# Two transformer blocks on one core: the RMS norms' sums, root and reciprocal in quarters, and the residual's add on VectorE

## The chip, the cores and the metric

One core of one Trainium2 chip. The metric is the device time of one execution in microseconds. The kernel before took 3231.95, 3235.20 and 3235.36 us in three runs, median 3235.2. All numbers of the trace come from one more execution, taken by the profiler.

## What is computed

The input is 1024 tokens of width 1024, all in fp32. The first block is an RWKV-7 mixer joined with differential attention, its output projection, a norm behind it, the residual, and a feed-forward with a short convolution between a norm before and a norm behind. The second block is a forgetting attention and a banded attention with gates, an output projection, a norm, and a feed-forward with a squared ReLU; a last norm ends it. What the change touches is the RMS norm over the 1024 features of a token:

```python
def rms_norm(x, g, eps=NORM_EPS):
    x32 = x.astype(jnp.float32)
    y = x32 * lax.rsqrt(jnp.mean(x32 * x32, axis=-1, keepdims=True) + eps)
    return (y * g.astype(jnp.float32)).astype(x.dtype)
...
        h = h + rms_norm(mix @ w_out[l], ln_attn_post[l])
        hn = rms_norm(h, ln_ffn_pre[l])
...
        h = h + rms_norm(f, ln_ffn_post[l])
```

## The kernel before

**Layout.** Activations lie feature-major: eight tiles (`KT`) of 128 features by 1024 tokens. A linear layer works in units: one unit is 128 output features, products over eight contraction tiles, 48 matmuls of 512 tokens, into one pair of PSUM banks (`bank2(slot)`; the two slots alternate, so unit n waits until unit n-2 is read out: `evac_done`). fp32 products are made of three matmuls on split operands: a rounded high part (`wh`, `xh`) and the rest (`wl`, `xl`), `three_products`, L359. For each unit SyncE loads a weight tile (`load_w`), ScalarE rounds it (`split_hi`, L330) and GpSimd subtracts (`split_lo`, L337), two units ahead at most.

**A norm's statistics.** There are six, numbered k = 0 to 5: before the first block (0), behind its output projection (1), before its feed-forward (2), behind it (3), before the second block (4), before the second feed-forward (5). Squares come from ScalarE (`square_act`, into `sq`). The sum over features is made in two ways. In 0, 2 and 4 TensorE multiplies each tile of squares by a 128x128 matrix of ones as it comes (`square_sum_pe`, L374) into banks 6 and 7, where every partition then holds the sums of all 1024 tokens. In 1, 3 and 5 VectorE adds the eight tiles into `ss` (`square_sum_dve`, L384) and TensorE multiplies `ss` once (`stat_products`, L415). ScalarE takes the root over 128x1024 (`stat_root_act`, L423) and VectorE the reciprocal in place (`stat_reciprocal`, L430), giving `rstd`. It is applied only when a unit is evacuated, or in a post norm to `y`.

**The post norms** (1 and 3) with the pre norm that follows (2 and 4) are one pipeline over eight tiles. VectorE multiplies `y` by gain and `rstd` (`post_scale`, L2265); GpSimd adds the residual tile `hres` into `src` (`post_norm_pool`, L2283), two buffers; ScalarE rounds it with the next gain into `xh` and squares it (`prep_act`, L394), and its queue issues the store of the new residual; VectorE makes `xl` (`prep_dve`, L404); SyncE loads `hres` two tiles ahead once an add is done (`post_norm_loads`, L2290). The add waits for the tile's scaling, the load, the store that still reads its buffer, and the low half and the square of two tiles before. TensorE runs the first unit of the next layer at the pace of the tiles, a tile's squares ahead of its products; the second unit follows whole. After the first pipeline GpSimd clears `y` by eight memsets, each after its add, before the feed-forward adds into it, and then splits the third unit's weights.

**Order.** Each engine's queue is written out by hand and is worked off in order; waits are on semaphores. After norm 4 the forget gate's unit (`U_FA`) is evacuated first and a chain of small operations on VectorE and ScalarE follows (L3102 to L3115) before the next unit's evacuation and weight split. Norm 5's products come behind a whole unit; the next two units have the transposes of the residual among their tiles (`turn_residual`, L2353), in banks 4 to 7.

Of the kernel before, what the change touches and what calls it, by code (L numbers as in the profile page):

```python
# [10 lines left out]
ALU = mybir.AluOpType  # L11
# [3 lines left out]
P = 128  # L15
T = 1024
D = 1024
# [92 lines left out]
def build_program(nc, a, out):  # L110
    ctx = ExitStack()
    with ctx:
# [20 lines left out]
        ones = at("ones", 205.75, [P, P])  # L133
# [7 lines left out]
        ss = at("ss", 200, [P, T])  # L141
        y = at("y", 112, [P, KT, T])
# [154 lines left out]
        stat_sum = sem("stat_sum")  # L297
        stat_root = sem("stat_root")
        rstd_ready = sem("rstd_ready")
# [115 lines left out]
        def stat_products(pe, sums):  # L415

            pe.wait_ge(ss_done, sums)
            for h in range(2):
                mm = nc.tensor.matmul(ps[:, 6 + h, :], ones[:, :], ss[:, h * HALF:(h + 1) * HALF],
                                      start=True, stop=True)  # L420
            mm.then_inc(stat_sum, 1)

        def stat_root_act(act, k, sums=None):  # L423


            act.wait_ge(*((ss_done, KT * (k + 1)) if sums is None else (stat_sum, sums)))
            nc.scalar.activation(rstd[:, :], bank2(3), ACT.Sqrt, bias=small[:, 0:1], scale=1.0 / D)\
                .then_inc(stat_root, 1)

        def stat_reciprocal(dve, k):  # L430
            dve.wait_ge(stat_root, k + 1)
            nc.vector.reciprocal(rstd[:, :], rstd[:, :]).then_inc(rstd_ready, 1)
            dve.wait_ge(rstd_ready, k + 1)
# [1829 lines left out]
        def post_scale(dve, kt, gain):  # L2263

            nc.vector.scalar_tensor_tensor(out=y[:, kt, :], in0=y[:, kt, :], scalar=col(gain, kt), in1=rstd[:, :],  # L2265
                                           op0=ALU.mult, op1=ALU.mult).then_inc(scaled, 1)

        def post_norm(dve, post_gain, r0, q0, pre_gain):
            post_scale(dve, 0, post_gain)
            for kt in range(KT):  # L2270
                if kt + 1 < KT:
# [926 lines left out]
```

## Time and profile before

| | |
|---|---|
| median of three runs | 3235.2 us |
| profiled execution, its own time | 3235.84 us |
| its span, first to last instruction | 3234.1 us |
| mean granted TensorE clock | 0.985 |
| busy: PE, PEld, DVE, ACT, POOL | 94%, 76%, 48%, 30%, 21% |
| the chain that ended last, share by engine | PE 83%, DVE 7%, issue 5%, ACT 2% |
| weights' high half on ScalarE (L335), mean | 1060 ns |
| weights' low half on GpSimd (L340), mean | 2444 ns |

PE is TensorE's matmuls, PEld its weight loads, DVE VectorE, ACT ScalarE, POOL GpSimd, SP SyncE. A row of a timeline gives the start, the length, engine, line, operation, output and inputs, shapes, count, and in brackets how long the engine was idle before it and what released it. Several instructions of one kind stand in one row, and the length then runs from the first start to the last end. The granted clock is a share of the full 2.4 GHz; 0.5 is the lower level of 1.2 GHz.

### The profile page before, as it was taken

The page shows a single profiled execution, that of the slowest core. Times are in us where ns is not written, and L with a number is a line of the kernel's source. Part 1 is how long each engine was busy: PE and PEld are TensorE (multiplying, and loading weights), DVE is VectorE, ACT ScalarE, POOL GpSimd, SP SyncE. Part 2 cuts the span into 40 slices and gives each one's busy share as a digit, 9 for nine tenths or more (in the row PEclk, how much of TensorE's full clock was granted, in tenths as well). Part 3 has the DMA queues.
Part 4 walks back from the last instruction along what each step waited for, and adds up shares of the span by engine and source line. Part 5 has one row for each costly group of instructions (what it writes and reads, how often), then busy time and mean ns, then how long its engine had stood idle before and what let it go on. Part 6 is the DMA issues. An engine that isn't in the chain of part 4 may idle for free.

```text
span 3234.1 us, 48488 instructions
## 1 busy us (share of the span) xinstructions
PE 3054.6 (94%) x20334; PEld 2444.8 (76%) x20334; DVE 1558.9 (48%) x1868; ACT 968.9 (30%) x1434; POOL 678.8 (21%) x292
## 2 busy tenths in 40 slices
PE   7999988889799999999799999999899999999998
PEld 5877767767488888888578877766688888888887
DVE  4156668741754444455731134555454444444455
ACT  3145545532322222222331133344332211111112
POOL 2410121212422122222243410000022221222221
PEclk9999999999899999999899999999899999999999
DMA  4443330021321111111243633344544411111111
GB/s 171 141 134 105 118 107 25 24 69 52 130 65 46 45 39 59 51 46 40 86 146 122 195 109 126 118 135 125 201 139 130 137 33 52 52 52 52 42 36 65
DMA packets 233982, 292.77 MB, mean 91 GB/s; under 512 B 10057, under 2 KB 182226, under 8 KB 233818
## 3 DMA queue, kind: packets, MB, share of 16 engines
q1 hardware_dynamic: 218842, 243.22, 24.5%
q10 hardware_dynamic: 14976, 47.19, 3.8%
q8 instruction: 124, 2.03, 0.3%
q14 instruction: 40, 0.33, 0.0%
HBM read 209.86 MB, written 80.51 MB: 90 GB/s over the span
## 4 chain that ended last, share of the span: by engine, by line
PE 83%; DVE 7%; issue 5%; ACT 2%; DMA 1%; POOL 1%; SPq 0%; DVEq 0%; ACTq 0%; POOLq 0%
PE ps L363 61%; PE ps L1331 4%; PE ps L1901 4%; PE ps L488 4%; PE ps L1971 2%; PE ps L1952 2%; PE ps L1929 1%; PE ps L1394 1%; DVE xl L404 1%; POOL src L2283 1%; PE ps L1932 1%; DVE y L2401 1%; DVE cb L2506 1%; PE ps L380 0%; PE ps L1372 0%
## 5 line engine op out<-in xcount | busy, mean ns | idle before, releaser
L340 POOL TENSOR_TENSOR wl<-wraw,wh 128x1024 fp32r<-128x1024 f32 x151 | 369.0, 2444 | 1638.1 <-ACT wh L335 1638.1
L363 PE MATMUL ps<-xh,wh 128*128 128x512 f32 x2192 | 686.4, 394 | 7.0 <-POOL xl L1169 2.2
L363 PE MATMUL ps<-xl,wh 128*128 128x512 f32 x2192 | 677.0, 390 | 0.0
L363 PE MATMUL ps<-xh,wl 128*128 128x512 f32 x2192 | 676.9, 390 | 0.0
L363 PEld LDWEIGHTS ps<-xh,wh 128*128 128x128 f32 x2192 | 412.4, 189 | 105.0 <-issue 8.1
L363 PEld LDWEIGHTS ps<-xl,wh 128*128 128x128 f32 x2192 | 413.2, 189 | 86.3
L363 PEld LDWEIGHTS ps<-xh,wl 128*128 128x128 f32 x2192 | 412.7, 188 | 86.3
L335 ACT ACTIVATE wh<-wraw 128x1024 fp32r<-128x1024 f32 x167 | 177.0, 1060 | 960.4 <-PE ps L363 894.3
L2401 DVE TENSOR_TENSOR y<-ps,y 128x1024 f32<-128x1024 f32 x208 | 253.2, 1222 | 241.6 <-PE ps L363 241.4
L2311 POOL TENSOR_TENSOR dl<-draw,dh 128x2048 fp32r<-128x2048 f32 x25 | 119.1, 4765 | 519.3 <-ACT dh L2307 519.3
L2448 DVE SCALAR_TENSOR_TENSOR cb<-ub,cols,cb 128x1024 f32<-128x1024 f32 x88 | 127.0, 1443 | 61.8 <-ACT cb L2484 56.0
L363 PE MATMUL ps<-dh,fh 128*128 128x512 f32 x480 | 149.3, 392 | 6.0 <-DVE y L2401 6.0
L363 PE MATMUL ps<-dh,fl 128*128 128x512 f32 x480 | 147.9, 389 | 0.0
L363 PE MATMUL ps<-dl,fh 128*128 128x512 f32 x480 | 147.9, 389 | 0.0
L2438 DVE TENSOR_TENSOR ub<-ps,rstd 128x1024 f32<-128x1024 f32 x44 | 53.9, 1225 | 172.7 <-PE ps L363 172.5
L2506 DVE TENSOR_TENSOR cb<-ps,rstd 128x1024 f32<-128x1024 f32 x32 | 39.2, 1225 | 193.4 <-PE ps L363 193.2
L2095 DVE CUSTOM_DVE_ANT_0 pbuf<-ps,bias 128x640 f32<-128x640 f32 (+7 forms) x128 | 85.5, 705 | 97.1 <-PE ps L1937 49.4
L2307 ACT ACTIVATE dh<-draw 128x2048 fp32r<-128x2048 f32 x25 | 47.8, 1913 | 235.2 <-PE ps L363 235.2
L1952 PE MATMUL ps<-ident,pbuf 128*128 128x128 f32 x528 | 94.0, 287 | 20.4 <-DVE pbuf L2151 9.8
L363 PEld LDWEIGHTS ps<-dh,fh 128*128 128x128 f32 x480 | 89.0, 188 | 29.4 <-DVE y L2401 11.5
L1952 PEld LDWEIGHTS ps<-ident,pbuf 128*128 128x128 f32 x528 | 60.9, 143 | 59.5 <-DVE pbuf L2151 17.3
L363 PEld LDWEIGHTS ps<-dh,fl 128*128 128x128 f32 x480 | 90.1, 188 | 18.9
(336 smaller groups left out, 4526.4 us busy)
## 6 DMA issues: line engine op xcount, KB each, us to landing
wraw<-in_w_up SPq DMA_DIRECT2D x76, 512.0 KB, 3.9
wraw<-in_w_in SPq DMA_DIRECT2D x67, 512.0 KB, 4.1
draw<-in_w_down SPq DMA_DIRECT2D x27, 1024.0 KB, 5.0
residual<-src ACTq DMA_DIRECT2D x32, 512.0 KB, 4.9
proj<-stage SPq DMA_DIRECT2D x30, 512.0 KB, 2.9
qk_hi<-hs ACTq DMA_DIRECT2D x24, 512.0 KB, 2.7
qk_lo<-ls SPq DMA_DIRECT2D x24, 512.0 KB, 2.8
kh<-qk_hi SPq DMA_DIRECT2D x48, 256.0 KB, 7.1
```

The lines of the kernel that those rows point to most:

```text
L335: nc.scalar.activation(wh[:, s, :, :], wraw[:, s, :, :], ACT.Copy).then_inc(w_hi, 1)
L340: nc.gpsimd.tensor_tensor(wl[:, s, :, :], wraw[:, s, :, :], wh[:, s, :, :].bitcast(F32), ALU.subtract).then_inc(w_lo, 1)
L363: mm = nc.tensor.matmul(ps[:, bank + h, :], w, x[:, h * HALF:(h + 1) * HALF], start=start and k == 0, stop=stop and k == 2)
L488: return nc.tensor.matmul(to, left, right, **kw)
L1331: ins = mm(ps[:, 2 * fill_slot(u) + h, :], w[:, s, kt, :], x[:, kt, h * HALF:(h + 1) * HALF], start=kt == 0 and part == 0, stop=kt == KT - ...
L1901: ins = mm(ps[:, 6 + h, :], w[:, s, kt, :], x[:, kt, h * HALF:(h + 1) * HALF], start=kt == 0 and part == 0, stop=kt == KT - 1 and part == 2)
L1952: ins = nc.tensor.transpose(ps[:, bank, (k - 4 * g) * P:(k - 4 * g + 1) * P], pbuf[:, (TT * b + n) % 3, m, k * P:(k + 1) * P], ident[:, :])
L2095: a2_dve.done(nc.vector.tensor_tensor_reduce(pbuf[:, step % 3, m, 0:size], ps[:, 2 * m:2 * m + 2, :].rearrange("p a n -> p (a n)")[:, 0:size],
L2311: nc.gpsimd.tensor_tensor(dl[:, :, :], draw[:, :, :], dh[:, :, :].bitcast(F32), ALU.subtract)\
L2401: nc.vector.tensor_tensor(y[:, m, :], bank2(2 + m % 2), y[:, m, :], ALU.add).then_inc(down_added, 1)
L2448: ff1_dve.done(nc.vector.scalar_tensor_tensor(out=cb[:, r, :], in0=ub[:, r, 2 - back:T + 2 - back], scalar=col_at("conv_w", (2 - back) * 2 ...
L2506: nc.vector.tensor_tensor(cb[:, 0, :], bank2((U_UP2 + t) % 2), rstd[:, :], ALU.mult)\
```

## The change

Sums: the ones become 128x32. Each tile of squares is multiplied in four matmuls of 256 tokens, each into its own 32 partitions of one bank (bank 4), so that partitions 32q to 32q+31 hold the sums of the q-th quarter of the tokens. Root and reciprocal then work on 128x256 (`root`). Two matrices with two rows of ones each, used by halves of 64 partitions, spread the quarters back to all partitions in banks 6 and 7 (`spread_pe`); in norms 0, 2, 4 and 5 ScalarE copies that to `rstd`, in the post norms VectorE multiplies from PSUM. In norms 1, 3 and 5 VectorE adds seven of the eight tiles; TensorE adds the last one in the bank. The residual's add, now with the post gain, moves from GpSimd to VectorE. Half of the second unit's tiles are issued among the first unit's. In norm 1 one weight split of ScalarE is moved behind the last square, in norm 2 one ahead of the copy. GpSimd's memsets wait for all sixteen low halves.

```diff
-        ones = at("ones", 205.75, [P, P])
+        spread_even = at("spread_even", 205.75, [P, P])
+        spread_odd = at("spread_odd", 207, [P, P])
+        ones = at("ones", 207.5, [P, 32])
+        root = at("root", 200, [P, T // 4])
...
+        STAT_BANK = 4
+        QUARTERS = [slice(32 * q, 32 * q + 32) for q in range(4)]
+        QUARTER_TOKENS = [slice(q * T // 4, (q + 1) * T // 4) for q in range(4)]
+        def quarter_sums(of, start, stop):
+            for q in range(4):
+                mm = nc.tensor.matmul(ps[QUARTERS[q], STAT_BANK, 0:T // 4], ones[:, :], of[:, QUARTER_TOKENS[q]],
+                                      start=start, stop=stop)
+            return mm
         def square_sum_pe(pe, q):
             if q and q % KT == 0:
                 pe.wait_ge(stat_root, q // KT)
             pe.wait_ge(x_sq, q + 1)
-            for h in range(2):
-                mm = nc.tensor.matmul(ps[:, 6 + h, :], ones[:, :], sq[:, q % 2, h * HALF:(h + 1) * HALF],
-                                      start=q % KT == 0, stop=q % KT == KT - 1)
-            mm.then_inc(ss_done, 1)
+            quarter_sums(sq[:, q % 2, :], q % KT == 0, q % KT == KT - 1).then_inc(ss_done, 1)
+        def post_sums_pe(pe, q):
+            pe.wait_ge(stat_root, q // KT)
+            pe.wait_ge(ss_done, q + KT - 1)
+            quarter_sums(ss, True, False)
+            pe.wait_ge(x_sq, q + KT)
+            quarter_sums(sq[:, 1, :], False, True).then_inc(ss_done, 1)
+        spread = bank2(3)
+        def spread_pe(pe, k):
+            pe.wait_ge(rstd_ready, k + 1)
+            for w, half in ((spread_even, 0), (spread_odd, 1)):
+                for r in range(2):
+                    mm = nc.tensor.matmul(ps[:, 6 + r, half * T // 4:(half + 1) * T // 4], w[ROWS[r], :], root[ROWS[r], :],
+                                          start=True, stop=True)
+            mm.then_inc(spread_done, 1)
+        def rstd_copy_act(act, k):
+            act.wait_ge(spread_done, k + 1)
+            nc.scalar.activation(rstd[:, :], spread, ACT.Copy).then_inc(rstd_copied, 1)
...
-            nc.scalar.activation(rstd[:, :], bank2(3), ACT.Sqrt, bias=small[:, 0:1], scale=1.0 / D)\
+            nc.scalar.activation(root[:, :], ps[:, STAT_BANK, 0:T // 4], ACT.Sqrt, bias=small[:, 0:1], scale=1.0 / D)\
...
-            nc.vector.reciprocal(rstd[:, :], rstd[:, :]).then_inc(rstd_ready, 1)
+            nc.vector.reciprocal(root[:, :], root[:, :]).then_inc(rstd_ready, 1)
+        def paced_units(pe, n, s, r0, q0, k):
...
+            for kt in range(KT):
+                square_sum_pe(pe, q0 + kt)
...
+                pe.wait_ge(x_lo, r0 + kt + 1)
+                mm = products(0, kt)
...
+                if 3 <= kt < KT - 1:
+                    products(1, kt - 3)
+            mm.then_inc(mm_done, 1)
+            for kt in range(4, KT):
+                if kt == 6:
+                    spread_pe(pe, k)
+                mm = products(1, kt)
+            mm.then_inc(mm_done, 1)
...
+        def post_scale(dve, kt):
+            nc.vector.tensor_tensor(y[:, kt, :], y[:, kt, :], spread, ALU.mult).then_inc(scaled, 1)
+        def post_add(dve, k, kt, gain, r0, q0):
+            s = kt % 2
+            dve.wait_ge(scaled, KT * k + kt + 1)
+            dve.wait_ge(h_loaded[s], 16 * (4 * k + kt // 2 + 1))
+            dve.wait_ge(x_lo, r0 + kt - 1)
+            dve.wait_ge(x_sq, q0 + kt - 1)
+            dve.wait_ge(src_stored[s], 16 * ((r0 + kt) // 2))
+            nc.vector.scalar_tensor_tensor(out=src[:, s, :], in0=y[:, kt, :], scalar=col(gain, kt), in1=hres[:, s, :],
+                                           op0=ALU.mult, op1=ALU.add).then_inc(added, 1)
+        def post_norm(dve, k, post_gain, r0, q0, pre_gain):
+            dve.wait_ge(spread_done, 2 * k + 2)
+            post_scale(dve, 0)
             for kt in range(KT):
+                post_add(dve, k, kt, post_gain, r0, q0)
                 if kt + 1 < KT:
-                    post_scale(dve, kt + 1, post_gain)
+                    post_scale(dve, kt + 1)
                 prep_dve(dve, r0 + kt, q0 + kt, pre_gain)
...
-            post_norm_pool(pool, 0, 8, 16)
+            pool.wait_ge(x_lo, 16)
             for kt in range(KT):
-                pool.wait_ge(added, kt + 1)
                 nc.gpsimd.memset(y[:, kt, :], 0.0).then_inc(y_zero, 1)
...
             stat_root_act(act, 0)
+            rstd_copy_act(act, 0)
...
-                split_hi(act, n + 2, n % 2)
+                if kt < KT - 1:
+                    split_hi(act, n + 2, n % 2)
...
-            stat_root_act(act, 1, 1)
+            split_hi(act, U_UP + 1, 1)
+            stat_root_act(act, 1)
             post_norm_act(act, 0, 8, 16, "ln_ffn_pre")
             stat_root_act(act, 2)
-            ff1_act_chunk(act, 0, 0)
+            split_hi(act, U_UP + 2, 0)
+            rstd_copy_act(act, 2)
+            ff1_act_chunk(act, 0, 0, begun=True)
...
+            stat_root_act(act, 4)
             split_hi(act, U_FA + 2, U_FA % 2)
-            stat_root_act(act, 4)
+            rstd_copy_act(act, 4)
...
-            for s in range(2):
-                unit_products(pe, s, s, 0, first=True)
+            unit_products(pe, 0, 0, 0, first=True)
+            unit_products(pe, 1, 1, 0, first=True, before=lambda kt: spread_pe(pe, 0) if kt == 4 else None)
...
-            stat_products(pe, 16)
-            unit_products(pe, U_UP, 0, 8, before=lambda kt: square_sum_pe(pe, 16 + kt))
-            for k in range(1, 4):
+            post_sums_pe(pe, 8)
+            spread_pe(pe, 1)
+            paced_units(pe, U_UP, 0, 8, 16, 2)
+            for k in range(2, 4):
                 unit_products(pe, U_UP + k, k % 2)
...
-            stat_products(pe, 32)
-            unit_products(pe, U_FA, 0, 16, before=lambda kt: square_sum_pe(pe, 32 + kt))
+            post_sums_pe(pe, 24)
+            spread_pe(pe, 3)
+            paced_units(pe, U_FA, 0, 16, 32, 4)
...
-            stat_products(pe, 48)
+            post_sums_pe(pe, 40)
+            def among(k, kt):
+                if k == 1 and kt == 2:
+                    spread_pe(pe, 5)
+                if kt % 2:
+                    turn_residual(pe, 4 * k - 4 + kt // 2)
...
+            for k, w in enumerate((spread_even, spread_odd)):
+                nc.vector.memset(w[:, :], 0.0).then_inc(spread_set, 1)
+                dve.wait_ge(spread_set, 3 * k + 1)
+                for r in range(2):
+                    row = 64 * r + 32 * k
+                    nc.vector.memset(w[row:row + 1, :], 1.0).then_inc(spread_set, 1)
```

In norm 5 `turn_residual` waits for the root before its first tile and for ScalarE's copy of the spread before its second. Where a norm's `rstd` is copied, VectorE waits for the copy (`rstd_copied`) behind its reciprocal.

## Rows read from the trace of the kernel before

**Rows 1.** The page's costliest groups, TensorE's first: busy, mean ns | idle before, releaser
```profile
L363 PE MATMUL ps<-xh,wh 128*128 128x512 f32 x2192 | 686.4, 394 | 7.0 <-POOL xl L1169 2.2
```

**Rows 2.** Busy time by stretch: PE, PEld, DVE, ACT, POOL (x), PEclk, DMA share, GB/s
```profile
804.40:826.60 22.20, 3.79 (x5) 1.18 (x4) 10.54 (x5) 5.36 (x6) 6.91 (x3) 0.58 0.02 1
...
826.60:859.00 32.40, 25.43 (x71) 14.03 (x72) 28.55 (x14) 15.56 (x15) 20.79 (x10) 0.92 0.80 269
...
863.60:874.50 10.90, 10.90 (x50) 9.03 (x49) 9.18 (x6) 2.31 (x2) 2.47 (x2) 1.00 0.17 50
```

**Rows 3.** Timeline, 806 to 827 us, all engines: start, length [idle before <-releaser]
```profile
807.59 1.47 DVE L392 TENSOR_TENSOR ss<-ss,sq 128x1024 f32<-128x1024 f32 x1 [9.34 <-ACT sq L372]
...
809.12 3.78 PE L419 MATMUL ps<-ss,ones 128*128 128x512 f32 x4 [4.71 <-DVE ss L392]
...
812.94 1.11 ACT L427 ACTIVATE rstd<-ps,small 128x1024 f32<-128x1024 f32 x1 [5.38 <-PE ps L419]
...
814.09 6.55 DVE L432 RECIPROCAL rstd<-rstd 128x1024 f32<-128x1024 f32 x1 [5.02 <-ACT rstd L427]
...
822.04 5.63 POOL L2283 TENSOR_TENSOR src<-y,hres 128x1024 f32<-128x1024 f32 x2 [14.05 <-DVE y L2265]
...
826.57 2.18 DVE L404 SCALAR_TENSOR_TENSOR xl<-src,cols,xh 128x1024 fp32r<-128x1024 f32 x1 [3.41 <-ACT xh L398]
```

**Rows 4.** Prices: durations ns min/median/max, a group's mean, and four timeline pieces
```profile
L979 DVE RECIPROCAL kb<-kb x16: 1694/1742/1753, 431.7 to 625.2; 128x256 f32<-128x256 f32 x16
...
L2081 ACT ACTIVATE pt<-ps 128x256 f32<-128x256 f32 x12 | 4.6, 385 | 20.6 <-PE ps L1952 20.6
...
L2438 DVE TENSOR_TENSOR ub<-ps,rstd x44: 1217/1225/1226, 870.1 to 1527.7; 128x1024 f32<-128x1024 f32 x44
...
L2265 DVE SCALAR_TENSOR_TENSOR y<-y,cols,rstd x16: 1270/1282/3398, 820.7 to 1617.1; 128x1024 f32<-128x1024 f32 x16
...
2520.08 1.88 PE L419 MATMUL ps<-ss,ones 128*128 128x512 f32 x4
...
1949.54 3.46 PE L1971 MATMUL ps<-pt,vt 128*64 128x256 f32 x32
...
471.63 0.69 PE L512 MATMUL ps<-wa,lora_w 64*128 64x512 f32 x1 [2.62 <-DMA lora_w<-in_w_iclr_up]
...
471.64 0.69 PE L517 MATMUL ps<-wa,lora_w 64*128 64x512 f32 x1
...
472.17 0.59 PE L512 MATMUL ps<-wa,lora_w 64*128 64x512 f32 x1
```

**Rows 5.** Timeline of TensorE and VectorE, 1576 to 1626 us
```profile
1576.65 3.78 PE L419 MATMUL ps<-ss,ones 128*128 128x512 f32 x4 [3.78 <-DVE ss L392]
...
1594.10 2.18 DVE L404 SCALAR_TENSOR_TENSOR xl<-src,cols,xh 128x1024 fp32r<-128x1024 f32 x1 [3.41 <-ACT xh L398]
...
1620.58 4.79 DVE L404 SCALAR_TENSOR_TENSOR xl<-src,cols,xh 128x1024 fp32r<-128x1024 f32 x2
```

**Rows 6.** Timeline at the loop of 826 us; releasers of the residual's adds (us, times)
```profile
857.74 1.28 DVE L404 SCALAR_TENSOR_TENSOR xl<-src,cols,xh 128x1024 fp32r<-128x1024 f32 x1 [3.45 <-ACT xh L398]
...
835.13 2.96 POOL L2283 TENSOR_TENSOR src<-y,hres 128x1024 f32<-128x1024 f32 x1 [1.76 <-DMA residual<-src]
...
  DMA residual<-src: 7.5, 3
```

**Rows 7.** Timeline behind the two loops: GpSimd, VectorE, TensorE
```profile
856.48 7.19 POOL L2773 MEMSET y<- 128x1024 f32 x8
...
1637.56 1.21 DVE L3102 TENSOR_TENSOR fa<-ps,rstd 8x1024 f32<-8x1024 f32 x1
...
1652.12 0.72 PE L363 MATMUL ps<-xh,wh 128*128 128x512 f32 x2 [1.57 <-DVE stage L3122]
```

**Rows 8.** The chain that ended last, 22 to 50 us: start, length, what
```profile
32.10 1.98 PE ps L380 x4
...
34.09 0.89 PE ps L2939 x8
```

More of the change, by code:

```diff
@@ L413, in apart, with stat_root_act @@
             eng.sem_inc(marks, 1)
[L415 to L426, printed above, removed]
-            nc.scalar.activation(rstd[:, :], bank2(3), ACT.Sqrt, bias=small[:, 0:1], scale=1.0 / D)\
+        def stat_root_act(act, k):
+            act.wait_ge(ss_done, KT * (k + 1))
+            nc.scalar.activation(root[:, :], ps[:, STAT_BANK, 0:T // 4], ACT.Sqrt, bias=small[:, 0:1], scale=1.0 / D)\
                 .then_inc(stat_root, 1)
@@ L2260, in build_program @@
         out_stored = sem("out_stored")
[L2263 to L2269, printed above, removed]
+        def post_scale(dve, kt):
[12 more added lines that the diff above has]
+            post_scale(dve, 0)
             for kt in range(KT):
+                post_add(dve, k, kt, post_gain, r0, q0)
                 if kt + 1 < KT:
-                    post_scale(dve, kt + 1, post_gain)
+                    post_scale(dve, kt + 1)
                 prep_dve(dve, r0 + kt, q0 + kt, pre_gain)
-        def post_norm_pool(pool, k, r0, q0):
-            for kt in range(KT):
-                s = kt % 2
-                pool.wait_ge(scaled, KT * k + kt + 1)
-                pool.wait_ge(h_loaded[s], 16 * (4 * k + kt // 2 + 1))
-                pool.wait_ge(x_lo, r0 + kt - 1)
-                pool.wait_ge(x_sq, q0 + kt - 1)
-                pool.wait_ge(src_stored[s], 16 * ((r0 + kt) // 2))
-                nc.gpsimd.tensor_tensor(src[:, s, :], y[:, kt, :], hres[:, s, :], ALU.add).then_inc(added, 1)
         def post_norm_act(act, k, r0, q0, pre_gain):
@@ L2408, in down_add @@
                         square_sum_dve(dve, squares + m - 1)
-            if squares is not None:
-                square_sum_dve(dve, squares + KT - 1)
         def y_squares_act(act, d, q0):
@@ L2930, in _ @@
             pe.wait_ge(lam_dve, 3)
-            nc.tensor.matmul(ps[:, 4, 0:1], ones[0:1, :], lam_dots[:, 2:3], start=True, stop=True).then_inc(lam_pe, 1)
+            pe.wait_ge(spread_set, 6)
+            nc.tensor.matmul(ps[:, 4, 0:1], spread_even[0:1, :], lam_dots[:, 2:3], start=True, stop=True).then_inc(lam_pe, 1)
+            pe.wait_ge(lam_dve, 4)
             for s in range(2):
@@ L3075, in _ @@
                 rwkv_dve(dve, j)
-            for kt in range(KT):
+            for kt in range(KT - 1):
                 square_sum_dve(dve, 8 + kt)
             stat_reciprocal(dve, 1)
-            post_norm(dve, "ln_attn_post", 8, 16, "ln_ffn_pre")
+            post_norm(dve, 0, "ln_attn_post", 8, 16, "ln_ffn_pre")
             stat_reciprocal(dve, 2)
+            dve.wait_ge(rstd_copied, 2)
             for s in range(2):
```

45 lines of the change are left out of this document (31 added, 14 removed).

## The prediction

> **What bounds the kernel now.** I read the page first. In [rows 1] TensorE's largest group of products waited 7.0 us in all over the whole span, so almost everywhere TensorE works without a gap, and only a change in TensorE's own work or in its few gaps can move the end. Next I asked for busy time by stretch at the norms. In [rows 2] the stretch from 804.4 to 826.6 us, after the last product of the output projection, has TensorE busy for 3.79 of 22.2 us; the next, to 859.0, has 25.43 of 32.4; and the one from 863.6 to 874.5, a whole unit, has 10.90 of 10.90. A unit is thus 10.9 us, one of its eight contraction tiles 1.36 us. The same shape comes back after the first block's feed-forward. So the change is argued in five places: the start, the two post norms with the pre norms that follow them, the fifth norm's tail, and the sixth norm.
>
> **The lead of a post norm.** The timeline [rows 3] is one chain, each row released by the one before. Products end at 804.41 (809.12 less its idle 4.71). ScalarE then splits a weight (1.06, its mean in the table of the profile), copies the tile and squares it, VectorE adds the last squares (807.59 to 809.06), TensorE sums over partitions (four passes, 3.78 us, so 0.94 each), ScalarE takes the root (1.11), VectorE the reciprocal (6.55), then scales; GpSimd adds the residual (two in 5.63 us); ScalarE rounds; the first low half starts at 826.57.
>
> The new prices. Reciprocal of 128x256: 1.74 us [rows 4]. Root from PSUM of 128x256: a ScalarE copy of that form takes 0.39; I take 0.45. Scaling from PSUM without a gain: 1.22. The add with gain on VectorE: 1.28, the undisturbed time of its form; that row's maximum, 3.40, belongs to instructions beside GpSimd's adds, which are gone. For the sums there is no 32-column row. Full-width plain fp32 takes 0.47 us per 512 columns at full clock (four passes in 1.88); eight passes of 256 are the same columns, so 1.9 us is the bound if the tiles do not run side by side. With 64-column tiles 32 passes took 3.46 us, 28 of them of 256 columns and four of 128; at the full-width rate the 7680 columns would take 7.1. Two tiles therefore do run beside each other, and four would give 0.45. I take 0.6 us with the last pass's latency, 1.1 at the low clock, near the lower end because of that factor of two. A gain below 0.45 is excluded by the streaming of 512 columns per tile. For the spread, the two 64-row tiles start together and the next pair follows 0.54 us later for 512 columns [rows 4]; four pairs of 256 lie between 1.1 (half of that each) and 2.2 (no gain from the halved width, weight loading binding), serial 1.9. I take 1.2 at the high level and 2.2 at the low one.
>
> Chain of the first post norm, from 804.41: with the weight split moved behind, ScalarE copies from 804.5 and squares until 806.6 (the add of 807.59 followed the square's old end; 1.0 earlier now). VectorE's seven earlier adds are in the bank already; TensorE adds the last tile, to 807.8. ScalarE is at the moved split until 807.6, so the root runs to 808.3, the reciprocal to 810.05, the spread to 812.3 (TensorE stood idle, and in the old lead it ran its sums at 0.94 us a pass), scaling to 813.6, the add to 814.9, rounding to 816.06. First low half at 816.1 against 826.57: **10.5 us** saved.
>
> Here a rule speaks against the change. No row shows a switch costing more than fractions of a microsecond: the 3.46 us above have full-width passes straight before and behind. The Trainium skill, TensorEngine Tiling (Array Packing), Key Properties, says that changing the tiling mode drains TensorE. By the rule each norm tile gets two drains more; by the row they cost under 0.2 us each and lie in TensorE's slack of the tile loop, so the sum stays as it is.
>
> Second post norm [rows 5]: products end at 1572.87 (1576.65 less 3.78). The eighth VectorE add ended at 1576.6, so the seventh, one of 1.3 us before it, at about 1575.3, as it still will, then two sets of sums (1577.3), root 1577.8, reciprocal 1579.6, spread 1581.8, scale 1583.1, add 1584.4, first low half 1585.6 against 1594.10: **8.5 us**.
>
> **The tile loop.** Before, from the start of the first low half to the end of the last: 826.57 to 859.02 and 1594.10 to 1625.37, or 32.4 and 31.3 us [rows 3, 5, 6]. In the new order VectorE does add, scale of the next tile, low half. The low half waits for ScalarE's rounding: add 1.28 + hand-over 0.04 + rounding 1.15 + 0.04, then 1.2 until the next add starts, so 3.7 us a tile; without that wait three operations would give 3.55. Seven of these and one low half: 27.2 us. Saved: **5.3 and 4.1 us**. What hides there: TensorE's sums (0.6) and one or two contraction tiles (1.36 or 2.72), at most 3.3 of 3.7. GpSimd is out of it. SyncE's loads of the residual now wait for VectorE's add, its issues and those of ScalarE's stores are as many as before. Their limit: a store issued at an add's end let the add two tiles later start 5.1 to 7.4 us on [rows 6]: the add at 835.13 waited 1.76 for a transfer issued at the end of the second add, 822.04 + 5.63 [rows 3]. At 3.7 a tile I allow 6.0; the 7.4 came from two stores and two loads issued within 2.4 us, so I take 5 to 6 and keep 7.4 as a bound (4.4 a tile).
>
> **The tails.** Call T the end of the last low half. Before, the first unit ended at 863.6, so TensorE started the third unit at 874.5, T + 15.45. Now four of the second unit's contraction tiles were done in the loop; left are the last sums (the last square ends at T - 0.3, the sums at 0.4), its tile (1.75), two tiles (4.5), the spread (5.7; root at 0.9 and reciprocal at 2.7 are ready by then), two tiles: T + 8.4. ScalarE's copy of the spread and VectorE's first evacuation end at 8.1. But GpSimd's eight memsets (7.19 us, [rows 7]) now wait for all sixteen low halves, where before they began with the last add, and the split of the third unit's weights (2.44, the mean in the table of the profile) is queued behind them: T + 9.75. That becomes the new bound, a TensorE wait of 1.3 us on GpSimd. Saved: **5.7 us**.
>
> At the second block the tail was from 1625.37 to 1652.12. It hangs on the forget-gate chain: its first multiply on VectorE at 1637.56, the third unit 14.56 later [rows 7]. The multiply now comes after the spread and its copy, T + 6.85, so the unit at T + 21.4 instead of T + 26.75: **5.3 us**. TensorE waits some 2 us there.
>
> **Start.** The loop over two tiles is copy, rounding, squares, sums 1.98, transposes 0.89 [rows 8], 6.3 us; with sums of 0.6 some 5.1, where VectorE (5.0: two copies of 1.23, two low halves of 1.28) and ScalarE (4.4: two of 1.15, two of 1.04) follow close. Two such periods give 2.4, the first tiles and the last sums 2 to 3, the spread inside the second unit costs 1.2, and a lower clock in the looser loop would take it all back (sums 1.1, transposes 1.8: 6.6 us). Between -1.5 and +5; I take **+2.5**. The added wait of ScalarE for the spread holds its weight split for the third unit back to some 19.7 us into the pair of units, low half 22.2, needed at 23.0: covered, narrowly. VectorE's six small memsets lie before the input's arrival.
>
> **Sixth norm.** One set of sums (1.75 as it delays the products, [rows 4]: 1.88) becomes two of 0.5 and a spread of 1.2: **-0.4**. Its ScalarE copy delays a weight split by about 3 us, with some 6 us to spare. Waiting for the copy before the second turned tile costs at most 0.3.
>
> **Sum.** 10.5 + 5.3 + 5.7 = 21.5; 8.5 + 4.1 + 5.3 = 17.9; + 2.5 - 0.4: 41.5 us. The profiled execution took 3235.84 us, 1.74 more than its span, and 0.6 above the runs' median of 3235.2; taken from it, 3194.3, so 3194.
>
> **Rivals.**
> - *The transfers bound the tile loops.* 4.4 us a tile instead of 3.7: 14 x 0.7 = 9.8 us less gain, 3204. For: the DMA engines' share was 0.80 at 269 GB/s in the old loop [rows 2], and 3.7 us a tile wants some 285. Against: only three adds of sixteen waited for transfers [rows 6], at the loops' beginnings, where two tiles followed each other closely. 15%.
> - *The 32-column tiles run one after the other*, the change not doing what it says. Sums then cost 1.9 (3.8 low): 2.7 and 5 more in the leads, four tiles a loop at 4.6 instead of 3.7 (7.2 in both), 1.3 each in the tails and 2.8 at the sixth norm, and the gain at the start is gone (2.5): 23 us less, 3217. The 64-column row speaks against. 10%.
> - *Slower.* Every switch between full-width, column-tiled and row-tiled matmuls stalls TensorE. About 60 switches; some 44 are not covered (the start's 16, the crowded tiles of the loops, leads and tails). It decides from 0.95 us each; at 1.2 the time is 3235.8 - 41.5 + 53 = 3247. The rows bound a switch at 0.2. It would be seen as gaps around the narrow passes. 3%, and 2% for no change.
> - 70% for the forecast, whose own range is 3186 to 3202: the start's -1.5 to +5, the spreads' bounds, 3.55 to 3.9 us a tile.
>
> A measurement of this kernel tells 0.2% (6.5 us) from no change. Faster: 0.95. The range takes in the forecast and the DMA rival with its own spread: 3184 to 3209; left out is mostly the serial case.
>
> **What would show it.** Right: low halves 3.6 to 3.8 us apart, the first ones 11.7 and 12.7 us after the products' end; narrow sums of about 0.6 us; a wait of TensorE on GpSimd's split behind the memsets; the third unit 36 to 37 us after the first low half. Wrong: sums of 1.9 us; VectorE's adds released by the residual's transfers; granted clock under 0.8 in the loops; a start loop still at 3.1 us a tile.

## The result, and the profile after

The changed kernel took 3197.68 us (median of four runs, 3195.33 to 3198.89); the kernel before, run beside it, 3233.57 (3228.49 to 3235.36). The ratio is 0.9891, interval 0.9874 to 0.9908. The profiled execution took 3198.89 us with a span of 3197.2 us and a mean granted clock of 0.987. The forecast was 3194: faster, as foreseen, and by 36.9 us between the two profiled spans where the sum was 41.5. One execution of the kernel before, beside the second set of the changed one, took 6135 us at full clock; it is left out of every comparison, and what held it up is not known.

Three names are used from here on. A *lead* runs from the end of the products in front of a post norm to the start of the first low half (`xl`, VectorE); a *loop* from there to the end of the last of the eight low halves, a moment called T; a *tail* from T to TensorE's third unit, or to that unit's counterpart in the second block.

First the stretches that answer to [rows 2]: busy time of PE, PEld, DVE, ACT, POOL, granted clock, DMA share and GB/s, in the lead, the tile loop and one unit behind it.

```profile
805.50:816.70 11.20, 3.27 (x24) 1.41 (x24) 5.42 (x5) 4.61 (x6) 2.34 (x1) 0.67 0.03 5
816.70:843.90 27.20, 23.75 (x130) 14.21 (x130) 25.40 (x21) 15.57 (x15) 0.00 (x0) 0.88 0.91 297
854.60:865.50 10.90, 10.90 (x50) 9.02 (x49) 8.50 (x6) 4.42 (x4) 2.53 (x1) 1.00 0.34 98
```

The lead of 22.2 us is 11.2, the loop of 32.4 is 27.2, and VectorE is now busy for 25.4 of those 27.2: with ScalarE's rounding, which stands between a tile's add and its low half, it sets the pace. Next the timeline of the lead, which answers to [rows 3]; products end at 805.48.

```profile
805.42 0.64 PE L386 MATMUL ps<-ss,ones 128*32 128x256 f32 x8
...
806.58 1.06 ACT L377 ACTIVATE sq<-y 128x1024 f32<-128x1024 f32 x1
...
807.69 0.64 PE L386 MATMUL ps<-sq,ones 128*32 128x256 f32 x8 [1.63 <-ACT sq L377]
808.49 0.45 ACT L455 ACTIVATE root<-ps,small 128x256 f32<-128x256 f32 x1
...
808.98 1.75 DVE L460 RECIPROCAL root<-root 128x256 f32<-128x256 f32 x1 [9.64 <-ACT root L455]
...
810.78 1.22 PE L412 MATMUL ps<-root,spread_even 64*128 64x256 f32 x4 [2.45 <-DVE root L460]
...
811.80 1.06 PE L412 MATMUL ps<-root,spread_odd 64*128 64x256 f32 x4
812.90 1.22 DVE L2319 TENSOR_TENSOR y<-y,ps 128x1024 f32<-128x1024 f32 x1 [2.18 <-PE ps L412]
814.16 1.28 DVE L2329 SCALAR_TENSOR_TENSOR src<-y,cols,hres 128x1024 f32<-128x1024 f32 x1
...
815.48 1.15 ACT L435 ACTIVATE xh<-src,cols 128x1024 fp32r<-128x1024 f32 x1 [6.54 <-DVE src L2329]
...
816.66 1.28 DVE L441 SCALAR_TENSOR_TENSOR xl<-src,cols,xh 128x1024 fp32r<-128x1024 f32 x1
```

The chain is the foretold one. Eight narrow passes take 0.64 us (at full clock), the root 0.45, the reciprocal 1.75 where the wide one took 6.55, the spread 2.08 at the low level. The first low half starts 11.18 us after the products' end; 11.7 was forecast.

Behind the loop, T is 843.85. The timeline of GpSimd and TensorE there, and then of the second block, where T is 1592.71:

```profile
843.91 7.23 POOL L2828 MEMSET y<- 128x1024 f32 x8 [32.92 <-DVE xl L441]
851.10 2.39 POOL L345 TENSOR_TENSOR wl<-wraw,wh 128x1024 fp32r<-128x1024 f32 x1
...
853.54 0.73 PE L368 MATMUL ps<-xh,wh 128*128 128x512 f32 x2 [1.05 <-POOL wl L345]
```

```profile
1585.22 1.28 DVE L2329 SCALAR_TENSOR_TENSOR src<-y,cols,hres 128x1024 f32<-128x1024 f32 x1 [1.01 <-DMA residual<-src]
...
1599.51 1.21 DVE L3183 TENSOR_TENSOR fa<-ps,rstd 8x1024 f32<-8x1024 f32 x1 [4.15 <-ACT rstd L419]
...
1611.96 2.32 DVE L3203 SCALAR_TENSOR_TENSOR stage<-ps,rstd 128x1024 f32<-128x1024 f32 x2
...
1614.32 0.72 PE L368 MATMUL ps<-xh,wh 128*128 128x512 f32 x2 [2.10 <-DVE stage L3203]
```

TensorE's unit starts at T + 9.69 after a wait of 1.05 us for GpSimd, and at T + 21.61 after one of 2.10 for the evacuation behind the forget-gate chain. In the second loop one add waited 1.01 us for a store of the residual.

All figures are us; a minus is a loss.

| step | before | after | saved | forecast |
|---|---|---|---|---|
| first lead (products' end to first low half) | 22.17 | 11.18 | 11.0 | 10.5 |
| first loop | 32.45 | 27.19 | 5.3 | 5.3 |
| first tail (T to the unit's start) | 15.45 | 9.69 | 5.8 | 5.7 |
| second lead | 21.23 | 11.86 | 9.4 | 8.5 |
| second loop | 31.27 | 28.29 | 3.0 | 4.1 |
| second tail | 26.75 | 21.61 | 5.1 | 5.3 |
| start (VectorE's evacuation near 90 us) | 90.29 | 88.59 | 1.7 | 2.5 |
| sixth norm (its last low half's end to the end of the span) | 720.0 | 720.4 | -0.4 | -0.4 |

The last row starts at the end of these low halves, 2514.10 before and 2476.74 after:

```profile
2511.85 2.25 DVE L404 SCALAR_TENSOR_TENSOR xl<-src,cols,xh 128x1024 fp32r<-128x1024 f32 x1 [1.22 <-ACT xh L398]
```

```profile
2474.50 2.24 DVE L441 SCALAR_TENSOR_TENSOR xl<-src,cols,xh 128x1024 fp32r<-128x1024 f32 x1 [1.22 <-ACT xh L435]
```

The rows give 11.0 + 5.3 + 5.8 + 9.4 + 3.0 + 5.1 + 1.7 - 0.4 = 40.9 us; the spans differ by 36.9. The missing part lies where the change has no line: 2.8 us from VectorE's evacuation near 90 us to the end of the output projection's products, 0.6 between the first tail and the second lead, and 0.4 between the second tail and the sixth norm. Windows over the same instructions in the first attention, before and after (columns as above):

```profile
249.50:257.20 7.70, 7.39 (x45) 5.84 (x45) 3.93 (x10) 4.50 (x13) 0.00 (x0) 1.00 0.06 18
296.90:324.00 27.10, 24.72 (x142) 19.23 (x142) 18.00 (x58) 17.17 (x44) 2.36 (x1) 1.00 0.13 40
```

```profile
247.80:257.10 9.30, 9.01 (x45) 7.11 (x45) 3.92 (x10) 4.48 (x13) 0.00 (x0) 0.82 0.05 15
296.80:325.40 28.60, 26.21 (x142) 20.31 (x142) 17.98 (x57) 17.10 (x43) 2.40 (x1) 0.94 0.13 38
...
1614.30:1627.10 12.80, 12.78 (x49) 10.43 (x50) 0.00 (x0) 2.01 (x2) 7.11 (x3) 0.87 0.80 237
```

The same 45 and 142 matmuls take 1.6 and 1.5 us longer, at a granted clock of 0.82 and 0.94 in place of 1.00: 3.1 us are lost there, more than the start had gained, and products of the output projection end at 805.48 where they ended at 804.40. The last line is the unit behind the second tail: 12.8 us where a unit takes 10.9 to 11.2, so 1.6 more, of which some 1.2 came back by the sixth norm. The 0.6 us between the first tail and the second lead stand in the second pair of traces below as well; their cause is open.

### The profile page after: what moved, and what is told of

It reads as the page before. It is cut to its first block, busy times and chain, and to the rows that moved or that the text cites. A ratio compares the mean times of both kernels' runs of the same rounds, so it can differ in the third digit from the quotient of the medians.

```text
span 3197.2 us, 48852 instructions
## 1 busy us (share of the span) xinstructions
PE 3035.5 (95%) x20514; PEld 2438.3 (76%) x20514; DVE 1526.2 (48%) x1887; ACT 968.2 (30%) x1438; POOL 634.5 (20%) x276
## 4 chain that ended last, share of the span: by engine, by line
PE 84%; DVE 6%; issue 5%; ACT 2%; DMA 1%; POOL 0%; DVEq 0%; ACTq 0%; SPq 0%; POOLq 0%
PE ps L368 62%; PE ps L1385 4%; PE ps L1955 4%; PE ps L542 4%; PE ps L2025 2%; PE ps L2006 2%; PE ps L1983 1%; PE ps L1448 1%; DMA residual<-src 1%; PE ps L1986 1%; DVE y L2459 1%; DVE cb L2563 1%; PE ps L1426 0%; DVE stage L2169 0%; DVE pbuf L2149 0%
```

## The experiments

Unless said otherwise an edit is made on the changed kernel, and T is again the end of a loop's last low half. Five questions were open: whether the slow attention belongs to the change, which of its parts earns what, what had stretched the old loop, whether the two waits behind the loops are worth anything, and what stands behind them.

**The changed kernel again**, no edit.

> The changed kernel once more, for its trace. The first profile lost 3.2 us against the kernel before between 250 and 325 us, in two stretches at the low granted clock behind waits of about 2 us that both kernels have, and 1.6 us behind the wait at 1614 us. Theory: whether such a wait is followed by a low stretch differs from one execution to the next, so this trace has the same waits, another set of low stretches outside the norms, and a time within 4 us of 3198; leads, loops and tails of the norms stay within 0.5 us (11.3, 27.2, T + 9.7; 11.9, 28.3, T + 21.6). Rival: the change itself causes the two low stretches in the attention, and they stand at the same places again.

3196.90 us (3196.67 to 3198.08), ratio 0.9884 [0.9867, 0.9902]. Low stretches of the clock lay at the same places of the first attention (granted clock 0.82 from 247.3 to 256.6 us). So of the two readings it was the one of a fixed loss that looked right, until the next run. Behind the second tail this execution kept full clock. The leads were 10.37 and 12.19 us, the loops 28.00 and 27.94, the tails 9.68 and 21.61: the tails repeat, but the leads and the first loop moved by 0.3 to 0.8 us, and the foretold 0.5 was too tight.

**The kernel before, again**, no edit, one execution.

> The kernel before once more, for a second trace. Open is whether the low granted clock near 250 and 310 us, which the changed kernel showed and the kernel before did not, is the change's or chance. If a fixed property of the two kernels: no low stretch between 240 and 370 us here, and one near 370 us as in the first trace. If chance: low stretches somewhere else in the first attention, with 1.6 us lost for each. Loops 32.4 and 31.3 us, third units 15.5 and 26.7 us behind them in either case.

3237.90 us, span 3236.2. Its window over the same 7.7 us:

```profile
249.50:257.20 7.70, 7.70 (x40) 6.36 (x39) 2.35 (x9) 2.91 (x9) 0.00 (x0) 0.78 0.02 5
```

The granted clock is 0.78 there and 0.94 from 296.9 to 324.0 us: the kernel before has these stretches too, only not in its first trace. Its products ended at 808.15 instead of 804.40, its first loop took 31.29 instead of 32.45. The 3.1 us are not the change's. Against this trace the second one of the changed kernel is 41.3 us shorter (3236.2 to 3194.9), against 36.9 for the first pair. The rows of the table give 38.9 us for this second pair (leads 11.8 and 8.8, loops 3.3 and 3.4, tails 5.4 and 5.2, start 1.6, sixth norm -0.5) and 40.9 for the first, so the places that the change touches are worth 39 to 41 us. The differences of the medians are 35.9 and 37.3 us in the two sets that hold both kernels; that they lie 2 to 5 us below the rows is not explained by any run.

**Without the second unit among the tiles.**

```diff
-            paced_units(pe, U_UP, 0, 8, 16, 2)
+            unit_products(pe, U_UP, 0, 8, before=lambda kt: square_sum_pe(pe, 16 + kt))
+            unit_products(pe, U_UP + 1, 1, before=lambda kt: spread_pe(pe, 2) if kt == 6 else None)
```

and the same for U_FA.

> The second unit is issued whole behind the first, the spread before its seventh contraction tile; all else as changed. Theory: four tiles of 1.36 us come back behind each loop: the first tail goes from T + 9.7 to T + 13.9 (1.3 us of it had been a wait on GpSimd anyway), the second from T + 21.6 to about T + 27, loops unchanged at 27.2 and 28: 9.5 us more, 3207. Rival: with the tiles in the loop TensorE delays the sums, so the loops get shorter without them and the time stays near 3198.

3207.62 us (3206.10 to 3210.07), ratio 0.9918 [0.9900, 0.9936]. Both loops took 27.17 us, the second tail 26.81. The interleaving costs the loop nothing. Behind it, it earns 5.2 us in the second tail, and behind the first loop 5.4 at the fifth unit (T + 37.25 here, T + 31.85 in the changed kernel); by the medians 10.7.

**The add back on GpSimd.**

```diff
-            nc.vector.tensor_tensor(y[:, kt, :], y[:, kt, :], spread, ALU.mult)
+            nc.vector.scalar_tensor_tensor(out=y[:, kt, :], in0=y[:, kt, :], scalar=col(gain, kt), in1=spread,
+                                           op0=ALU.mult, op1=ALU.mult)
...
-            nc.vector.scalar_tensor_tensor(out=src[:, s, :], in0=y[:, kt, :], scalar=col(gain, kt), in1=hres[:, s, :],
-                                           op0=ALU.mult, op1=ALU.add)
+                nc.gpsimd.tensor_tensor(src[:, s, :], y[:, kt, :], hres[:, s, :], ALU.add)
```

> The residual's add goes back to GpSimd, VectorE scales with the gain from PSUM; sums, quarters, spread and pacing as changed. Theory: VectorE's instructions beside GpSimd's adds take up to 3.4 us again and the loops 32.4 and 31.3 us instead of 27.2 and 28.3, each lead 2.0 more: 12 us more, 3210. Rival: the old loop was long because TensorE's wide sums and the transfers held it; with narrow sums it stays at 27 to 29 and only the leads cost 4 us in all, 3202.

3205.01 us (3198.79 to 3210.19), ratio 0.9913 [0.9896, 0.9931]. The time lies between the two that were foretold, and its executions are 11 us apart; the loops decide, and for the rival: 28.21 and 28.78 us, not 32.4 and 31.3. The 8 us lie in the leads (12.35 and 13.26, 2.6 together), in 1.5 of the loops and in tails about 2 us longer each. The line of the scaling shows what is different (min/median/max in ns):

```profile
L2319 DVE SCALAR_TENSOR_TENSOR y<-y,cols,ps x16: 1266/1269/1280, 807.8 to 1586.6; 128x1024 f32<-128x1024 f32 x16
```

Beside GpSimd's adds no scaling is stretched, where in [rows 4] the longest took 3398 ns. It reads the factor from PSUM now. The low halves, whose operands all lie in SBUF, still are: up to 2.84 us in the two loops, against 1.28.

**Both undone:** the two edits above in one kernel, so that sums, root and reciprocal in quarters, and the read from PSUM, are what is left.

> Both of the above: only the sums, root, reciprocal and spread are as changed. Theory: against the kernel before it gains in the leads (8.9 and 7.4), the first tail (1.5) and the start (1.7), some 19 us, so 3215 to 3217; the parts add up, as the add and the pacing work at different places. Rival: they overlap, the loop of 4.5 us a tile leaving TensorE so idle that pacing or not makes no difference: then this is within 3 us of the run with the add alone moved back.

3213.99 us (3211.19 to 3215.01), ratio 0.9937 [0.9919, 0.9955]; loops 28.50 and 28.15 us. The parts left are worth 20 us of the 37 between the medians; the add's move and the interleaving 17 together. Taken back singly they cost 8 and 11, taken back when the other is already gone 6 and 9, so they nearly add up, as foretold.

**GpSimd's add with the factor in SBUF.** On the version with the add on GpSimd:

```diff
-            ..., in0=y[:, kt, :], scalar=col(gain, kt), in1=spread,
+            ..., in0=y[:, kt, :], scalar=col(gain, kt), in1=rstd[:, :],
...
             stat_root_act(act, 1)
+            rstd_copy_act(act, 1)
```

and the same for norm 3.

> The version with the add back on GpSimd and nothing else, but the scaling of the post norms reads the spread factor from a ScalarE copy in SBUF instead of from PSUM. Open is why the version with GpSimd's add took 28.2 and 28.8 us a loop where the kernel before takes 32.4 and 31.3. Theory: what stretched the old loop is VectorE's scaling with two operands in SBUF beside GpSimd's adds. Then most of the scalings take about 3.4 us again, GpSimd's adds 3 us, the loops 31 to 32.5 us each, each lead 1.1 us longer by the copy: 2 x 1.1 + 3 to 7 us more than the 3205.0 of the version that reads PSUM: 3210 to 3215. Rival: the half of the second unit among the tiles, or the shorter sums, shortened the loop. Then scalings stay near 1.27 us, the loops at 28 to 29, and the time is 3207.

3217.63 us (3215.70 to 3220.30), ratio 0.9945 [0.9928, 0.9961], 12.6 above the version that reads PSUM, where 5 to 9 were foretold. In the traces 5.7 of these lie in the loops and 4.7 in the leads, some 2.1 of them ScalarE's two copies; the rest is within the 11 us between executions of the other version. Its line of the scaling and its timeline in the loop:

```profile
L2319 DVE SCALAR_TENSOR_TENSOR y<-y,cols,rstd x16: 1271/1282/3420, 817.9 to 1604.5; 128x1024 f32<-128x1024 f32 x16
```

```profile
836.29 1.27 DVE L441 SCALAR_TENSOR_TENSOR xl<-src,cols,xh 128x1024 fp32r<-128x1024 f32 x1
837.49 3.40 DVE L2319 SCALAR_TENSOR_TENSOR y<-y,cols,rstd 128x1024 f32<-128x1024 f32 x1
841.03 3.38 DVE L441 SCALAR_TENSOR_TENSOR xl<-src,cols,xh 128x1024 fp32r<-128x1024 f32 x1
844.33 1.27 DVE L2319 SCALAR_TENSOR_TENSOR y<-y,cols,rstd 128x1024 f32<-128x1024 f32 x1
```

```profile
836.44 3.36 POOL L2330 TENSOR_TENSOR src<-y,hres 128x1024 f32<-128x1024 f32 x1 [2.36 <-DVE y L2319]
840.97 2.35 POOL L2330 TENSOR_TENSOR src<-y,hres 128x1024 f32<-128x1024 f32 x1 [1.16 <-DVE y L2319]
```

The loops are 31.33 and 31.34 us, as in the kernel before. Two neighbours on VectorE take 3.4 us each, one after the other, while GpSimd's add runs, and 1.27 otherwise. Not most of the scalings are stretched, as was expected, but six of sixteen, and six in each trace of the kernel before. Within the loop only one operand's place was changed, and the old loop came back. By the Trainium skill, GPSIMD Engine Reference, Key points, GpSimd shares its SBUF interfaces with VectorE and contends with its instructions that have two SBUF inputs; these rows agree, 1.27 us from PSUM against up to 3.42 from SBUF.

**Each memset behind its add**, as before the change.

```diff
-            pool.wait_ge(x_lo, 16)
             for kt in range(KT):
+                pool.wait_ge(added, kt + 1)
```

> GpSimd's eight memsets of y wait each for its tile's add again, as before the change, instead of for all sixteen low halves. Theory: they are done within the loop, the split of the third unit's weights ends earlier, and the third unit starts at T + 8.4 instead of T + 9.7: 1.3 us less, no wait of TensorE on GpSimd there. Rival: memsets beside VectorE's additions with two inputs stretch these as GpSimd's adds did (3.4 instead of 1.28), up to 2 us a tile: the first loop then takes up to 40 us and the time grows by 10 us.

3197.43 us (3196.55 to 3198.50), ratio 0.9880 [0.9863, 0.9897]: nothing that can be told from the changed kernel. The expectation's rival is out: the memsets, 0.96 us each beside VectorE's rows, stretch none of them (adds and low halves of the loops took at most 1.29 us). The wait at T + 9.7 is gone, but the fifth unit shows another (timeline of TensorE; T is 843.64):

```profile
875.45 0.73 PE L368 MATMUL ps<-xh,wh 128*128 128x512 f32 x2 [1.34 <-POOL wl L345]
```

That is T + 31.81. In the changed kernel this unit starts at 875.70, T + 31.85, without a wait. Its weights' low half is queued on GpSimd behind that of a down projection (4.62 us), which hangs, through ScalarE's and VectorE's work on the first two units, on the copy of the spread. The wait for the memsets lay in front of a second chain as long as itself.

**The spread one contraction tile earlier** (`if kt == 5` in `paced_units`), one execution.

> The spread inside the paced pair stands before the second unit's sixth contraction tile instead of its seventh. Theory: the second tail hangs on the forget gate's chain, which starts with the spread, so T + 21.6 becomes T + 20.2; the first tail hangs on GpSimd and stays at T + 9.7. 1.4 us less in all. Rival: the second tail hangs on the third unit's weights, and both stay.

3196.33 us. The second tail fell from 21.61 to 20.41, where 20.2 was foretold, so it hangs on the forget gate's chain; the wait left is 0.90 us, for GpSimd's split. The first tail kept its wait, 1.02 us at T + 9.68.

**The next unit's split and evacuation ahead of the forget-gate chain's second half.**

```diff
             rstd_copy_act(act, 4)
+            split_hi(act, U_QKV2 + 2, U_QKV2 % 2)
...
             nc.vector.tensor_scalar(cneg[:, :], fa[:, :], 0.0, None, ALU.min).then_inc(fa_dve, 1)
+            dve.wait_ge(mm_done, U_QKV2 + 1)
+            stage_free(dve, 0)
+            nc.vector.scalar_tensor_tensor(out=stage[:, 0, :], in0=bank2(U_QKV2 % 2), scalar=0.125, in1=rstd[:, :],
+                                           op0=ALU.mult, op1=ALU.mult).then_inc(evac_done, 1)
...
```

> Behind the second loop VectorE evacuates the second unit while the forget gate's chain waits for ScalarE, and ScalarE rounds the third unit's weights ahead of that chain's work; otherwise as changed. Theory: TensorE no longer waits 2.1 us there and the low stretch of the clock behind that wait (1.6 us) goes as well: the unit that starts at T + 21.6 starts at T + 19.3, and the time falls by 2.3 to 3.9 us. Rival: the chain's end is needed elsewhere soon after, and the gain is given back before the attention.

3201.52 us (3200.45 to 3205.35), ratio 0.9891 [0.9873, 0.9908]. No wait at T + 21.6, but one of 2.32 us for GpSimd's split at T + 32.73. The foretold gain of 2.3 to 3.9 us did not come: as its rival said, the wait came back 11 us later. That the time is 4 us above the changed kernel's says little, since the output projection's products, ahead of the edit, already ended 6 us late in this trace, at 811.62, and the ratio to the kernel before in the same set is that of the changed kernel.

**Both of these edits together** (the memsets and the chain).

> Both of these edits together. Theory: 1.3 + 2.3 to 3.9 us, so 3192 to 3195, faster than both kernels. Rival: no difference from the changed kernel beyond its scatter of some 4 us from run to run, which is as large as the gain.

3197.68 us (3192.40 to 3201.67), ratio 0.9875 [0.9855, 0.9894]: within the scatter of the changed kernel. Both later waits stand, 1.30 us at T + 31.85 and 2.52 at T + 32.92. Two rows name what is behind the second, ScalarE's split of that unit and SyncE's issue of the gate's store:

```profile
1622.97 1.06 ACT L340 ACTIVATE wh<-wraw 128x1024 fp32r<-128x1024 f32 x1 [12.19 <-DMA wraw<-in_w_in]
```

```profile
1602.28 0.81 SPq L2684 DMA_DIRECT2D rel_d<-rel  x1
1603.13 8.28 SPq L333 DMA_DIRECT2D wraw<-in_w_in  x2
1613.03 6.98 SPq L2688 DMA_DIRECT2D cneg_d<-cneg  x1
```

ScalarE waited 12.19 us for weights whose load stands on SyncE's queue behind `rel_d`, a store of 768 KB; the next issue took 6.98 us.

**The version above with that store six loads later and the spread at tile 5.**

```diff
-                if u == 2:
+                if u == 8:
                     sp.wait_ge(rel_filled, 1)
...
-                if kt == 6:
+                if kt == 5:
                     spread_pe(pe, k)
```

(The expectation says four loads later; the edit makes it six. The spread's place moves the chain by 1.2 us, as the run above showed, and has no part in SyncE's order.)

> The changed kernel with four edits: GpSimd's memsets each behind their add, the next unit's split and evacuation ahead of the forget-gate chain's second half, the spread one contraction tile earlier, and the 768 KB store of the relative bias issued four weight loads later on SyncE's queue. Open is why the version with the first two edits gained nothing: its wait moved to 33 us behind the second loop (2.5 us). Theory: there the fourth unit's weights landed late, behind that store and the stores that wait for the forget gate. Then the wait of 2.5 us at 33 us is gone, TensorE has no wait over 0.5 us in the 45 us behind the second loop, and the time is 3 to 4 us below the changed kernel, near 3194. Rival: the weights wait for the chain itself through SyncE's store of the scan's result, which stays where it was; then a wait of 1 to 2.5 us stays at 31 to 34 us and the time is 3196 to 3198. Behind the first loop the earlier spread takes the fifth unit's weights some 1.3 us forward: no wait at 31.8 us there, where the version with the first two edits had 1.3 us.

3194.66 us (3193.80 to 3198.74), ratio 0.9879 [0.9862, 0.9895]. TensorE shows no wait in the 35 us behind either loop. The split that had waited 12.19 us for its load, and the issue of the gate's store that had taken 6.98:

```profile
1613.90 1.06 ACT L340 ACTIVATE wh<-wraw 128x1024 fp32r<-128x1024 f32 x1 [2.68 <-PE ps L368]
```

```profile
1613.45 0.30 SPq L2688 DMA_DIRECT2D cneg_d<-cneg  x1
```

VectorE's evacuation of the fourth unit behind the first loop came at T + 30.45 instead of 32.72, and that of the unit behind the second wait at T + 30.45 instead of 32.82 (second trace of the changed kernel, whose unit ran at full clock). In those two places this version is 4.6 us ahead of the changed kernel; by the medians it is 2.2 to 3.0 us below the two sets of the changed kernel, from which the intervals don't part it.

## Why the prediction held, and where it didn't

*Bound and places.* TensorE's gaps at the norms were the place to gain, and the norms gave 39.6 us (22.1 and 17.5) where 39.4 was forecast. Sums, root, reciprocal and spread cost what the nearest rows had said: 0.64 (0.6), 0.45 (0.45), 1.75 (1.74), 2.08 (2.2) at the low level and 1.1 (1.2) at the high.

*Leads.* Right, 0.5 and 0.9 us on the careful side. The sums had been allowed 1.0 to 1.1 us a set for the low level; they ran at 0.64 in the first lead, and in the second both sets took from 1555.10 to 1556.17. How much of this one gets depends on when the clock falls: over the eight traces whose leads have the same instructions, the first lead is 10.4 to 11.2 us and the second 11.9 to 12.7.

*Tile loops.* Seven periods of 3.70 us and one low half of 1.28 are 27.2, which the first loop has (27.19). The second took 28.3, one add waiting 1.01 us for a store: the transfers' rival at the size of one tile, not of seven. It comes and goes: ten of the sixteen loops in the eight traces with the add on VectorE have one such wait and take 27.7 to 28.5 us, six have none and take 27.2. Their mean is 27.75, so the loops' term was some 0.6 us too good on the average. The DMA engines' share in the loop was 0.91 at 297 GB/s (0.80 at 269 before).

*The reason for the loops* holds as far as it goes, and is incomplete. The prediction said of the longest scaling, 3.40 us, that it "belongs to instructions beside GpSimd's adds, which are gone". The traces bear this out: scalings are stretched only beside these adds. What the prediction missed is that the factor's move to PSUM, which it took for a detail of the spread, does most of it alone. With the add on GpSimd and the factor in PSUM the loops were 28.2 and 28.8 us; with the factor in SBUF 31.3 and 31.3. So with the add on GpSimd the operand's place is worth some 3 us a loop, and the add's move then 0.5 to 1 there and the rest of its 8 us in leads and tails. The fourth combination, the add on VectorE with the factor in SBUF, was not run; whether the add's move alone would have given the same loop is open.

*Tails.* The first is the foretold wait on GpSimd (1.05 against 1.3 us), the second the foretold chain (21.61 against 21.4; "some 2 us" of wait, 2.10). The prediction called the first of them the new bound, and one would credit its removal with its length. That was not so: each wait taken away came back 11 to 22 us later (2.32 and 1.34 us), because another chain of the same length stood behind it.

*Start.* Mis-sized: 1.7 against 2.5 (1.6 in the second pair of traces), within the stated -1.5 to +5. The chain there reads:

```profile
30.28 0.64 PE ps L386 x8
30.92 1.04 PE ps L3002 x8
...
33.25 4.51 DMA residual<-src
...
41.28 1.01 PE ps L386 x8
42.29 7.80 PE ps L368 x28
```

The first products start at 42.29 instead of 46.69, a gain of 4.4, inside the foretold "2.4 and 2 to 3", though the last tile waited for a store of the residual, which the prediction did not count. But the unit behind them ran at the low level (1.4 us, from a granted clock of 0.87 over the 11 us from 42 us) and the spread took its 1.1. That leaves 1.9.

*Sixth norm.* Right: a loss of 0.4 us was forecast, and from its last low half to the end the changed kernel takes 0.4 us more in the first pair of traces and 0.5 in the second. Two sets of sums (2482.82 to 2483.90) and a spread (2487.70 to 2488.84) take 2.2 us of TensorE where one set took 1.88.

*The clock elsewhere* has no term in the sum. In the first pair of traces it took 3.1 us of the first attention and 1.6 behind the second tail, and the places without a line of the change lost 3.8 us net, which is within 0.2 the distance from 40.9 to 36.9. In the second pair the same places gained 2.4 us, from 38.9 to 41.3. That the forecast of 3194 came within 4 us of 3197.7 is therefore partly luck: such places move by more than that between two traces.

*The rivals.* Serial tiles: out, eight narrow passes take 0.64 us, not 1.9. Stalls at switches: out. In a full-clock piece of the loop,

```profile
842.84 0.62 PE L368 MATMUL ps<-xh,wl 128*128 128x512 f32 x2
843.54 0.64 PE L386 MATMUL ps<-sq,ones 128*32 128x256 f32 x8
844.11 0.73 PE L368 MATMUL ps<-xh,wh 128*128 128x512 f32 x2
844.68 0.62 PE L368 MATMUL ps<-xl,wh 128*128 128x512 f32 x2
```

the first narrow pass waited for the square, which ScalarE ended at 843.48. So the way into the narrow passes does not show here; only the way out does. From the narrow passes' start to the next start are 0.57 us, 0.1 more than the 0.47 that 512 columns of plain fp32 take, and the first two full-width passes then take 0.57 from start to next start where later pairs take 0.46. (They do so at 853.54 too, behind a plain wait.) The way in can be read where nothing is waited for, at the spread:

```profile
847.42 0.62 PE L368 MATMUL ps<-xl,wh 128*128 128x512 f32 x2
847.87 0.62 PE L368 MATMUL ps<-xh,wl 128*128 128x512 f32 x2
848.42 0.70 PE L412 MATMUL ps<-root,spread_even 64*128 64x256 f32 x4
```

0.55 us pass between the last two starts where 0.45 is usual, so 0.1. The drain weighed in the prediction thus costs some 0.1 us on the way in and 0.1 to 0.2 on the way out, within the 0.2 a switch that the prediction had as its bound.

## What to carry to other kernels

Ask of each VectorE operation that runs beside GpSimd where its operands lie: with the add on GpSimd, a factor left in PSUM was worth some 3 us in each loop of eight tiles, and 2 to 3 in each lead, a copy of 1.0 included. A wait that a trace shows is worth only its distance to the next chain; look up what is due one and two units later, and what stands on the queue that feeds it, before crediting it. Where two traces of one kernel disagree by some us in a part that no edit touches, take a second trace before giving that part a cause.

## What was not expected of the hardware

One execution of the kernel before had full clock at 250 and 310 us, another had 0.78 and 0.94 there, over the same instructions. In the stretch before the slow one TensorE had been busy for 2.96 of 5 us (245 to 250 us) in the trace that stayed fast and for 2.94 in the changed kernel's, which fell: a gap alone did not decide it. Over all thirteen traces the low stretch near 310 us is missing only in the first of the kernel before, which was thus the exception and not the rule; the one near 250 us stands in five. Over the eleven traces of the versions made from the changed kernel, whose work up to there is the same but for the start, the output projection's products ended between 800.4 and 811.6 us: after 805.4 in the five that also have a low stretch near 370 us, before 805.1 in the six that have none there. Edits of 2 us are therefore read from the stretch in which they lie, not from the total.
